# First mixer of a fused two-block transformer kernel: which banks the latent queries wait for, and in which steps the grouped heads are prepared

## The reference

```
h = rms_norm(x) @ w_in                       # cut into latent, differential and grouped columns
q_a = rms_norm(rms_norm(c_q) @ w_uq), k_a = rms_norm([rms_norm(c_kv) @ w_ukv, k_rope])   # 6 latent heads
q_b, k_b = rope(rms_norm(..))                # 4 differential heads, two maps each
q_c, k_c = axial_rope(rms_norm(..))          # 6 grouped query heads, 2 key heads
o_a = softmax(q_a k_a) v_a
o_b = rms_norm((softmax_0 - lam * softmax_1) v_b)
o_c = softmax(q_c k_c) v_c
x = x + [o_a, o_b, o_c] @ w_o
x = x + (silu(xn @ gate) * (xn @ up)) @ w_down
```

## Time and profile before

| | us |
|---|---|
| three runs, median (lowest to highest) | 2429.31 (2427.16 to 2429.71) |
| the profiled execution's own time | 2429.67 |
| its span, first to last instruction | 2427.9 |
| granted TensorE clock over the span, mean | 0.975 |
| TensorE busy in the span | 2297.4 (95%) |
| VectorE / ScalarE busy | 1709.6 (70%) / 1477.7 (61%) |

### The profile page before, as it was taken

How to read it: one execution, slowest core, us unless ns; L and a number is a source line. 1 busy time by engine, 2 the same in 40 slices (tenths; PEclk the granted TensorE clock), 3 DMA queues, 4 the chain that set the end, 5 groups by cost and what they waited for, 6 DMA issues and landing times.

```text
span 2427.9 us, 31711 instructions
## 1 busy us (share of the span) xinstructions
PE 2297.4 (95%) x11904; PEld 1954.8 (81%) x11904; DVE 1709.6 (70%) x2358; ACT 1477.7 (61%) x2121; POOL 238.4 (10%) x142
## 2 busy tenths in 40 slices
PE   6889999978999999999999899999999999999997
PEld 5777887877788899788799778888888888888885
DVE  5754555773555645655653669999999999998998
ACT  4554444554544455444455558777777777777776
POOL 0421000232000241100224000000000000000000
PEclk9989999999999999999999989999999999999998
DMA  7314554522555644555553369999999999999996
GB/s 256 128 44 139 192 187 157 196 70 74 184 187 188 198 130 132 169 187 191 184 164 127 130 208 360 356 362 351 359 357 355 356 354 356 356 363 347 366 347 239
DMA packets 156989, 570.92 MB, mean 235 GB/s; under 512 B 18528, under 2 KB 18880, under 8 KB 156192
## 3 DMA queue, kind: packets, MB, share of 16 engines
q1 hardware_dynamic: 153744, 555.58, 65.0%
q0 software_dynamic: 3088, 13.27, 1.6%
HBM read 567.72 MB, written 1.05 MB: 234 GB/s over the span
## 4 chain that ended last, share of the span: by engine, by line
PE 88%; DVE 8%; ACT 2%; issue 1%; POOL 1%; DMA 0%; SPq 0%; DVEq 0%; POOLq 0%; ACTq 0%
PE bank L487 24%; PE bank L489 24%; PE bank L488 24%; PE bank L1828 2%; PE bank L1829 2%; PE bank L1830 2%; PE bank L847 2%; PE bank L1477 2%; PE bank L2297 1%; PE bank L825 1%; DVE w_lo L428 1%; PE bank L2318 1%; PE bank L704 1%; DVE X L1716 1%; DVE small L792 0%
## 5 line engine op out<-in xcount | busy, mean ns | idle before, releaser
L428 DVE TENSOR_TENSOR w_lo<-raw,w_hi 128x1024 fp32r<-128x1024 f32 x986 | 1189.8, 1225 | 314.4 <-ACT w_hi L422 287.2
L422 ACT CAST w_hi<-raw 128x1024 fp32r<-128x1024 f32 x1055 | 1101.7, 1051 | 344.3 <-PE bank L489 288.8
L487 PE MATMUL bank<-w_hi,x_hi 128*128 128x512 f32 (+2 forms) x2592 | 1022.1, 394 | 19.5 <-DVE x_lo L1740 7.9
L489 PE MATMUL bank<-w_hi,x_lo 128*128 128x512 f32 (+2 forms) x2592 | 1003.4, 387 | 0.0
L488 PE MATMUL bank<-w_lo,x_hi 128*128 128x512 f32 (+2 forms) x2592 | 1002.4, 387 | 0.0
L487 PEld LDWEIGHTS bank<-w_hi,x_hi 128*128 128x128 f32 x2592 | 492.2, 190 | 113.2 <-POOL w_lo L428 8.5
L489 PEld LDWEIGHTS bank<-w_hi,x_lo 128*128 128x128 f32 x2592 | 491.1, 189 | 97.5
L488 PEld LDWEIGHTS bank<-w_lo,x_hi 128*128 128x128 f32 x2592 | 492.5, 190 | 89.8
L428 POOL TENSOR_TENSOR w_lo<-raw,w_hi 128x1024 fp32r<-128x1024 f32 x69 | 165.1, 2398 | 537.8 <-ACT w_hi L422 532.9
L1698 POOL TENSOR_TENSOR small<-small 128x1 f32<-128x1 f32 x10 | 9.2, 916 | 1170.4 <-ACT small L1694 1170.3
L1828 PE MATMUL bank<-x_hi,w_hi 128*128 128x256 f32 x384 | 110.7, 288 | 0.0
(11 more groups left out here) (231 smaller groups left out, 1851.6 us busy)
## 6 DMA issues: line engine op xcount, KB each, us to landing
raw<-in_stream SPq DMA_DIRECT2D x1055, 512.0 KB, 5.8
tab<-in_lngb POOLq DMA_DIRECT2D x5, 1024.0 KB, 8.2
arena<-in_rpb POOLq DMA_DIRECT2D x16, 256.0 KB, 7.0
tab<-in_rowv POOLq DMA_DIRECT2D x2, 640.0 KB, 9.0
X<-in_x SPq DMA_DIRECT2D x1, 1024.0 KB, 5.1
out_y<-X SPq DMA_DIRECT2D x2, 512.0 KB, 2.6
tab<-in_ropec POOLq DMA_DIRECT2D x2, 448.0 KB, 5.0
tab<-in_ropes POOLq DMA_DIRECT2D x2, 448.0 KB, 7.3
```

The costliest lines, as they stand in the source:

```text
L422: nc.scalar.copy(w_hi[:, s % SPLIT, :], raw[:, slot, :]).then_inc(hi_done, 1)
L428: e.tensor_tensor(w_lo[:, s % SPLIT, :], raw[:, s % RAW, :], w_hi[:, s % SPLIT, :].bitcast(F32), ALU.subtract).then_inc(done, 1)
L487: pe.matmul(out, xh, wh, start=first, stop=False)
L489: return pe.matmul(out, xl, wh, start=False, stop=last)
```

## The change

1. The latent queries wait for `acc_act` and `acc_dve` of one evacuation less: only for the chunks that held banks 4 to 7, not for the latent keys and values.
2. The halves of `gq` run in steps 0, 2, 3 and 4 with the evacuation in step 5 (before: 0, 2, 4, 6 and 7). Those of `gkv` run in 6 and 8 with the evacuation in 9 (before: 8, 9 and 10).
3. `grouped` has four parts instead of two or three: squares, sums, rotation, final product. The queries' parts run in steps 5, 6, 7, 8 (before: 8 and 9), the keys' in 9, 10, 11, 12 (before: 11 and 12). Two `drain_dve` calls go.
4. The second `diff_norm` uses another part of the scratch `sc_mla`, and the waits for inverse roots name their own count.
5. Latent units alternate between banks 4 and 5 from step 6 on. The wait for the `gq` evacuation moves from step 8 to step 6. The wait of `gkv` for a unit goes.

```diff
@@ -1046,8 +1046,8 @@
 
                     e.wait_ge(qk_lo, E.qk.at())
                     if b0 == 4:
-                        wait(e, acc_act, E.acc.at())
-                        wait(e, acc_dve, E.acc.at())
+                        wait(e, acc_act, E.acc.at(-1))
+                        wait(e, acc_dve, E.acc.at(-1))
                 for hx in range(kn):
                     def use(wh, wl, hx=hx):
                         for c in range(2):
@@ -1200,23 +1200,23 @@
                     rsqrt(E, at, TB * h)
                 if part == 1 and c == C_GQ:
                     rows_made["gqa"] = E.rs.at()
+                if part == 2 and c == C_GQ and E.kind == "dve":
+                    E.link(crossed(E, x, h, f, turns, z, 0))
+                if part == 3 and c == C_GQ:
                     if E.kind == "dve":
-                        E.link(crossed(E, x, h, f, turns, z, 0))
                         E.link(e.tensor_tensor(x, x, over_heads(CT[:, :, f:f + GD], h), ALU.mult))
                         e.tensor_tensor(x, x, z, ALU.add).then_inc(qk_src, 1)
-
-                        drain_dve(E)
                     E.qks.n += 1
-                if part == 1 and c == C_GK and E.kind == "dve":
+                if part == 2 and c == C_GK and E.kind == "dve":
                     E.link(turned(E, x, h, f, turns, heads_view(y, h, GD), z, 0))
                     E.link(e.tensor_tensor(heads_view(y, h, GD), heads_view(y, h, GD), z, ALU.add))
-                if part == 2 and c == C_GK:
+                if part == 3 and c == C_GK:
                     if E.kind == "dve":
-                        need_rs(E)
+                        need_rs(E, rows_made["gk"])
                         e.tensor_tensor(x, heads_view(y, h, GD), scales(at, h, GD), ALU.mult).then_inc(qk_src, 1)
-
-                        drain_dve(E)
                     E.qks.n += 1
+                if part == 1 and c == C_GK:
+                    rows_made["gk"] = E.rs.at()
 
             def diff_norm(h0, part):
 
@@ -1226,7 +1226,8 @@
                 a = MH * MV + h0 * DV
                 x3 = O[:, :, a:a + n * DV]
                 x = x3.rearrange("p t (h d) -> p t h d", h=n)
-                y = sc_mla[:, 0:TB * n * DV]
+                y0 = TB * GH * GD if h0 else 0
+                y = sc_mla[:, y0:y0 + TB * n * DV]
                 if part == 0:
                     drain_dve(E)
                     squares(E, (y.rearrange("p (t n) -> p t n", t=TB), x3))
@@ -1236,9 +1237,11 @@
                         sums(E, at, n, DV, y)
                         mean(E, at, TB * n, DV, False).then_inc(ms_ready, 1)
                     rsqrt(E, at, TB * n)
+                if part == 1:
+                    rows_made[h0] = E.rs.at()
                 if part == 2:
                     if E.kind == "dve":
-                        need_rs(E)
+                        need_rs(E, rows_made[h0])
                         e.tensor_tensor(x, x, scales(at, n, DV), ALU.mult).then_inc(qk_src, 1)
                     E.qks.n += 1
 
@@ -1306,11 +1309,10 @@
                     h = step - 6
                     if E.kind == "pe":
                         e.wait_ge(qk_src, made["mla"])
-                        if step == 8:
+                        if step == 6:
                             e.wait_ge(acc_act, E.acc.at())
                             e.wait_ge(acc_dve, E.acc.at())
-                    bk = 6 + step % 2 if step < 8 else 4 + step % 2
-                    unit(E, bk, pair_of(place(2 * h), 2, MQK), [blk(QA, h * MQK, MQK), blk(KA, h * MQK, MQK)], w=MQK,
+                    unit(E, 4 + step % 2, pair_of(place(2 * h), 2, MQK), [blk(QA, h * MQK, MQK), blk(KA, h * MQK, MQK)], w=MQK,
                          lag=2)
                     ready[h] = E.qk.at()
                 if step == 11:
@@ -1343,39 +1345,32 @@
             gq, gkv = column_halves(5, 4), column_halves(6, 6)
 
             def fill(step):
-                if step in (0, 2, 4, 6, 7):
+                if step in (0, 2, 3, 4, 5):
                     if step == 0 and E.kind == "pe":
                         wait(e, acc_act, E.acc.at())
                         wait(e, acc_dve, E.acc.at())
                     next(gq, None)
-                if step in (8, 9, 10):
-                    if step == 8 and E.kind == "pe":
-                        e.wait_ge(qk_lo, ready[1])
+                if step in (6, 8, 9):
                     next(gkv, None)
                 if step >= 14:
                     out_half(step - 14)
                 if step < 5:
                     latent_heads(step)
                     made["mla"] = E.qks.at()
-                if step in (6, 7, 8):
-                    if step == 8:
-                        grouped(0, C_GQ, GH, F_GQ, at_g)
-                    else:
-                        diff_norm(0, step - 6)
+                at_gk = at_g + TB * GH
+                if step in (5, 6, 7, 8):
+                    grouped(step - 5, C_GQ, GH, F_GQ, at_g)
+                    made["gq"] = E.qks.at()
+                if step in (6, 7):
+                    diff_norm(0, step - 6)
                 if step == 9:
-                    grouped(1, C_GQ, GH, F_GQ, at_g)
-                    made["gq"] = E.qks.at()
                     diff_norm(0, 2)
                     made["diff01"] = E.qks.at()
-                if step in (10, 11):
+                if step in (10, 11, 12):
                     diff_norm(DH // 2, step - 10)
-                if step == 11:
-                    grouped(0, C_GK, GKV, F_GK, at_g + TB * GH)
-                if step == 12:
-                    diff_norm(DH // 2, 2)
                     made["diff23"] = E.qks.at()
-                    grouped(1, C_GK, GKV, F_GK, at_g + TB * GH)
-                    grouped(2, C_GK, GKV, F_GK, at_g + TB * GH)
+                if step in (9, 10, 11, 12):
+                    grouped(step - 9, C_GK, GKV, F_GK, at_gk)
                     made["gk"] = E.qks.at()
 
             def rows(at, n):
```

## The result

The changed kernel takes 2435.01 us (median of 9 runs, 2433.8 to 2436.45). The kernel before takes 2428.02 (9 runs on the same chips, 2425.18 to 2429.71). The ratio is 1.0029, 95% interval 1.002 to 1.0038: slower by 7.0 us, a little more than the 0.2% that can be told from no change. The profiled execution took 2435.98, with a span of 2434.2 and a mean granted clock of 0.973.

The account below looks back on a forecast made before the run. VectorE's queue was taken to set the pace, its two-operand instructions held by GpSimd's subtractions. +0.8 us (chunk 4) and +2.4 (attention steps) made +3.2 on 2429.67: 2432.9, adjusted to 2432.5; 8-in-10 range 2421.5 to 2437.

Parts of the forecast that it names:

- the bound that I had called no change: Whole kernel: 0.2% (4.9 us, 2424.4 and 2434.2) is what can be told from no change.
- Part A: Latent queries' wait around chunk 4: hold on L979 delays the copy out; +0.1 us in layer 0, +0.7 in layer 1.
- Part B: Attention steps 3 to 12, paced by VectorE: 52.68 us becomes 53.85, +1.2 us a layer, +2.4 in both.
- The four terms that I gave for step 8: Attention step 8: 3.25 + 0.96 + 2.26 + 0.9 = 7.35 us, with POOL's `gkv` subtraction holding L1206.
- All holds: VectorE instructions using two big on-chip memory operands, or writing such results, stand still until POOL's 2.36 us subtraction ends.
- the second one in step 3: Step 3, `latent_heads(3)`: POOL's added `gq` subtraction holds VectorE a second time, 2.3 us.
- TensorE's new waits: Attention: waits of 2 to 3 us appear in steps 5, 6 and 10; step 11's 5.1 us shrinks to about 1.
- a sign of being wrong: VectorE pauses between steps 6 and 12 longer than the 0.5 to 1.2 us behind ACT.
- the 52.68 us of the steps before: Sum of attention steps 3 to 12 before the change, from layer 0's times between L792 instructions.
- The three waits: Rival: TensorE's three targeted waits in both layers come back in full, 27.8 us, 2401.5 us; chance 0.04.
- The rival without new holds: No new holds in chunk 4, step 3 and step 8: -8.4 us, 2420.9 us; chance 0.12.
- The rival in which TensorE is too slow in step 6: Lower clock after idle time delays step 7's scores: at full price +2.3 us a layer, 2437.1 us; chance 0.15.

Follow-up runs that it names:

- delay_before: Kernel before plus three VectorE additions of 1024 columns (results unused) ahead of layer 1's residual sum: 2431.62 us, ratio 1.0017.
- a_only: Kernel before with only the latent queries' wait shortened by one evacuation: 2428.37 us against 2427.79, ratio 1.0005.
- b_only: Changed kernel with the latent queries' shorter wait undone, the attention edits kept: 2433.23 us, ratio 1.0019 to the kernel before.
- short_two: Changed kernel with POOL subtracting only 32 of 1024 columns in two halves per layer, those of steps 3 and 8: 2425.22 us, ratio 0.9985 to the kernel before.
- short_after: Changed kernel with POOL subtracting only 32 of 1024 columns of each of its halves in the first two mixers: 2410.84 us, ratio 0.9933 to the kernel before.
- gated_after: Changed kernel with VectorE doing some POOL subtractions, POOL's of steps 6 and 8 waiting for row maxima, ScalarE's rounding and copying out earlier: 2417.04 us.
- short_before: Kernel before with POOL subtracting only 32 of 1024 columns of each of its halves in the first two mixers: 2418.45 us, ratio 0.9962.
- gated_before: Kernel before with VectorE doing subtractions of steps 0, 2, 4 and 9, POOL's of 6 and 8 waiting for maxima, ScalarE's rounding and evacuation earlier: 2422.05 us.
- gated_no1: `gated_after` with the latent queries waiting for the whole layer's banks again: 2416.92 us, ratio 0.9956 to the kernel before.

## Why the prediction was right, and where it was off

The mechanism was right and the size too small: 2435.0 against 2432.5, inside the range, but past the bound that I had called no change.

*Part A.* As forecast: the wait gone, a wait of 3.14 us (forecast about 3.4) ahead of the second half, L979 at 3.40 from 81.37 (forecast about 3.4 from 81.4), transposes at 86.86 (forecast 87), the start of step 0 moved by +0.1 us. The last figure is in part luck: `delay_before` has the same code up to there as the kernel before, and its step 0 begins at 94.74 against 96.37. In layer 1 the same place gave +1.1 instead of +0.7. The transposes came 0.7 later, as forecast, but the second half and the transposes ran at the lower clock (0.63 us a matmul throughout, 0.97 us the first four transposes instead of 0.60). `a_only` puts the part at +0.6 in the medians.

*Part B.* The step lengths, from one maximum to the next: steps 3 and 4 12.56 us (forecast 12.7), steps 5 to 8 21.63 (22.1), steps 9 to 12 19.37 (19.05), together 53.56 (53.85; 53.89 measured in layer 1). The four terms that I gave for step 8 add up to 7.37 and not to 7.35, and it took 7.14. All holds came where they were placed, and with their length: the second one in step 3, L1208 at 3.00 us, L670 at 1.82. Only step 10 came out longer than read (4.63 us), since L664 waits 0.78 us for ScalarE's square in it. Of TensorE's new waits, those in steps 5 and 10 came as forecast (2.79 and 3.45 us), the one in step 6 is 0.38, and one of 2.37 in step 13 was not foreseen; the one in step 11 kept 0.62 us (forecast about 1). Since VectorE sets the pace, none of this moved the sum. VectorE's pauses behind ScalarE in steps 11 and 12 were 1.35 and 1.36 us, just over the 1.2 that I had named as a sign of being wrong; the kernel before has 1.48 and 1.36 in the same steps, so the sign was set too tight.

*The term that was mis-sized* is what stood on the other side of that subtraction, the 52.68 us of the steps before. I took it from layer 0 of one execution. Its step 6 is the odd one. VectorE's timeline of the kernel before, in layer 0 and in layer 1:

```profile
120.31 0.68 DVE L792 TENSOR_REDUCE small<-bank 128x2 f32<-128x512 f32 x1
126.59 0.69 DVE L792 TENSOR_REDUCE small<-bank 128x2 f32<-128x512 f32 x1 [1.81 <-PE bank L489]
...
513.69 0.68 DVE L792 TENSOR_REDUCE small<-bank 128x2 f32<-128x512 f32 x1
518.54 0.69 DVE L792 TENSOR_REDUCE small<-bank 128x2 f32<-128x512 f32 x1 [1.29 <-PE bank L489]
```

TensorE over the same two stretches (busy time, then the granted clock, the DMA share and GB/s):

```profile
120.30:126.60 6.30, 6.07 (x31) 0.74 0.20 69
513.70:518.50 4.80, 4.58 (x31) 1.00 0.27 90
```

The same 31 matmuls took 6.3 us at a mean clock of 0.74 and 4.8 at full clock. VectorE waits for TensorE in this step, so the step is TensorE's and its length goes with the clock. The code of it is the same in `a_only` and `delay_before`, and there it took 4.82 to 4.85 us in all four layers. So 51.6 was the usual sum, and B is 53.85 - 51.6 = 2.25 a layer, 4.5 in both, not 2.4. That is the failed step: "In all 52.68 becomes 12.7 + 22.1 + 19.05 = 53.85, so +1.2 us a layer". The same execution stood 1.65 us over the median of nine runs, not 0.36 as over the first three; that the odd step made it so is likely but not shown. With 51.6 and the median of nine the sum is 2428.0 + 0.8 + 4.5 = 2433.3, and `b_only`, the part by itself, has +5.4 measured against 4.5.

*The rivals.* The three waits did not come back in full (2401.5 was forecast for that). The rival without new holds did not happen, but `short_two` and `short_after` show that it would have been a gain, with 9.8 and 24 us under the changed kernel (`short_after` takes away the old holds too). The rival in which TensorE is too slow in step 6 met its condition in part: from 120.3 to 126.6 the changed kernel had a mean granted clock of 0.50, which is 1.2 GHz throughout. In layer 0 it still did not decide: the maximum at 130.39 has no idle time ahead of it, because VectorE had been held until just before. In layer 1 it did by a little: VectorE waited 0.32 us for TensorE ahead of that maximum, and step 6 took 6.70 us instead of 6.45. The price named in the rival was 2.3.

*The rule of the Trainium skill* (GPSIMD Engine Reference, Key points), that GpSimd and VectorE contend where VectorE has two SBUF inputs, bore out for L979 (1.22 us became 3.40) and L1208 (0.96 became 3.00), where no row of before could show it.

*Still open* are 1.7 us of the 7.0 (2435.0 against the mended 2433.3). Behind the first mixers the changed kernel's profile falls back by 2.9 us against that of before, in stretches whose code is the same: 1.4 us near 620 us, 1.4 near 1012 and 0.3 further on. From 605 to 625 the mean granted clock is 0.91 in it and 1.00 in the kernel before. `b_only` shows no such loss and `a_only` shows both steps. But edit 1 does not go with it. From the first maximum of step 13 in layer 1 to the end of the span, seven of the thirteen profiles take 1874.3 to 1875.0 us and six take 1876.5 to 1877.1 (`delay_before` without its 3.7), and none lies between. Three of the six kernels with edit 1 are among the long ones (the changed kernel, `a_only`, `gated_after`) and three of the seven without it (`short_before`, `gated_before`, `delay_before`). The kernel before and the changed one fell on different sides. How often each kernel falls on which side is not known from one profile each.

## What to carry to other kernels

Before you add work of an engine beside another, list which instructions of the pacing engine run while it has the memory both share; moving 2.4 us of GpSimd work next to two-operand VectorE work cost 2.0 to 2.2 us each time, and a wait that puts the same work beside VectorE's bank reads made it free. A wait in an engine's list is worth only what the engine behind it can deliver sooner: 5.2 us taken away gave no gain that the medians show, held or not. When a forecast subtracts two sums of step lengths, take the sum of before from every layer that runs this code and use the one that repeats, with the granted clock of each step beside it. And a place in time read from one profile carries the luck of everything ahead of it: the same code reached step 13 of layer 1 at 553.6 us in one profile and at 548.1 in another.

## What the runs showed of the hardware

- The hold goes both ways. A two-operand VectorE instruction of 0.2 to 1.2 us grew to 1.8 to 3.4 us, until POOL's 2.36 us subtraction had ended. POOL's grew to 3.25 and 2.79 us where VectorE's was under way.
- A VectorE instruction with one operand on 12 numbers (L670, 0.17 us) is held too and takes 1.82 us. A sum over 768 columns (L664) or a maximum from a bank (L792) beside the same subtraction is not.
- After idle time of 3.1 us in the middle of a chunk TensorE's matmuls of 512 columns took 0.63 us (1.2 GHz) and not 0.40: in `gated_after` for 3.5 us right behind it, in the changed kernel's layer 0 for 3.5 us that began 1.1 us behind it (82.57 to 86.1), in its layer 1 throughout the half (475.8 to 481.2). Behind the wait of 5.19 us in another place of `gated_no1` the query matmuls took 0.44 us instead of 0.29 for 3.5 us; behind the one of 5.16 us in the kernel before it was 4.7 us.
